# Input rows normalized tile by tile, token halves outermost in the input product, h2 taken ahead of the output sums, and a new list of items for the mixed part

## What is computed

```python
h = rms_norm(x, attn_norm)
proj = h @ w_in                                  # 1024 RWKV columns, then q, k, v of 12 heads, 4 forget logits
y_rwkv = rwkv7_group(proj[..., :1024], ...)      # recurrence over tokens, 4 heads x 64
y_fox  = softmax attention with forget gates     # 4 heads
y_moba = softmax attention on chosen key blocks  # 4 heads
y_sb   = stick-breaking attention                # 4 heads
x = x + concat(y_rwkv, y_fox, y_moba, y_sb) @ w_out
h2 = rms_norm(x, mlp_norm)
x = x + square(relu(h2 @ w_mlp_up)) @ w_mlp_down
```

## Time and profile before

| | us |
|---|---|
| three timed runs, median (lowest to highest) | 1093.09 (1090.01 to 1093.42) |
| the profiled execution | 1084.01 |
| its span, first to last instruction | 1082.4 |
| PE busy in it | 1000.0 (92%) |
| DVE busy | 401.9 (37%) |
| ACT busy | 346.3 (32%) |
| mean granted PE clock | 0.973 |

### The profile page before, as it was taken

The page is one execution under the profiler, slowest core; times in us unless marked ns, Lnnn a source line. Parts: engine busy times, 40 slices in busy tenths (PEclk is TensorE's granted clock), DMA queues, the critical chain, the costliest instruction groups (busy, mean ns, idle before and its releaser), DMA issues.

```text
span 1082.4 us, 20333 instructions
## 1 busy us (share of the span) xinstructions
PE 1000.0 (92%) x8560; PEld 770.7 (71%) x8560; DVE 401.9 (37%) x758; ACT 346.3 (32%) x608; POOL 56.0 (5%) x108
## 2 busy tenths in 40 slices
PE   3999999898997988889969998999999999999998
PEld 3775666556895856566634447999877799997776
DVE  3005142834566565554381125332212142221212
ACT  3001331411333166675460113544211134441110
POOL 0000000112410000002420000000000000000000
PEclk9999999899998899999979998999999999999999
DMA  9011111002000358557988202222122243211222
GB/s 350 23 59 60 59 59 59 33 33 99 7 5 2 92 206 277 161 176 232 348 355 289 91 1 78 79 78 79 39 78 78 78 132 98 84 39 40 81 93 108
DMA packets 57005, 117.46 MB, mean 109 GB/s; under 512 B 4891, under 2 KB 27963, under 8 KB 56787
## 3 DMA queue, kind: packets, MB, share of 16 engines
q1 hardware_dynamic: 50674, 93.05, 25.5%
q0 software_dynamic: 6240, 23.12, 6.2%
HBM read 109.62 MB, written 6.53 MB: 107 GB/s over the span
## 4 chain that ended last, share of the span: by engine, by line
PE 87%; DVE 6%; issue 3%; ACT 2%; DMA 2%; SPq 1%; DVEq 0%; ACTq 0%
PE PS L735 12%; PE PS L1144 11%; PE PS L1145 11%; PE PS L1146 11%; PE PS L817 7%; PE PS L721 6%; PE PS L1114 5%; PE PS L982 3%; PE PS L1217 3%; PE PS L1050 2%; PE PS L1004 2%; PE PS L945 2%; PE PS L739 2%; DMA AR<-in_cache_kv 1%; PE PS L960 1%
## 5 line engine op out<-in xcount | busy, mean ns | idle before, releaser
L2045 DVE TENSOR_TENSOR WL<-Wraw,WH 128x2048 fp32r<-128x2048 f32 x32 | 73.4, 2293 | 164.2 <-ACT WH L1449 164.2
L1144 PE MATMUL PS<-h2H,WH 128*128 128x288 f32 x448 | 132.8, 296 | 0.0
L1145 PE MATMUL PS<-h2L,WH 128*128 128x288 f32 x448 | 132.2, 295 | 0.0
L1146 PE MATMUL PS<-h2H,WL 128*128 128x288 f32 x448 | 131.7, 294 | 0.0
L735 PE MATMUL PS<-W,HM 128*128 128x384 f32 (+1 forms) x384 | 127.2, 493 | 0.0
L1449 ACT ACTIVATE WH<-Wraw 128x2048 fp32r<-128x2048 f32 x32 | 61.0, 1907 | 163.8 <-DMA Wraw<-in_w_mlp_down 140.8
L735 PEld LDWEIGHTS PS<-W,HM 128*128 128x128 f32 x384 | 73.5, 192 | 51.0 <-issue 1.8
L1144 PE MATMUL PS<-WH,uH 128*128 128x512 f32 x256 | 101.4, 396 | 1.8 <-issue 1.8
L1145 PE MATMUL PS<-WL,uH 128*128 128x512 f32 x256 | 99.8, 390 | 0.0
L1146 PE MATMUL PS<-WH,uL 128*128 128x512 f32 x256 | 99.6, 389 | 0.0
L1146 PEld LDWEIGHTS PS<-h2H,WL 128*128 128x128 f32 x448 | 84.4, 188 | 0.0
(11 more groups left out here) (311 smaller groups left out, 1343.4 us busy)
## 6 DMA issues: line engine op xcount, KB each, us to landing
AR<-in_cache_kv SPq DMA_DIRECT2D x76, 384.0 KB, 4.1
AR<-in_cache_kv POOLq DMA_DIRECT2D x44, 384.0 KB, 4.8
Wraw<-in_w_mlp_up SPq DMA_DIRECT2D x16, 1024.0 KB, 5.4
Wraw<-in_w_mlp_down SPq DMA_DIRECT2D x16, 1024.0 KB, 4.9
W<-in_w_in SPq DMA_DIRECT2D x5, 1536.0 KB, 6.5
VQ<-in_x_prompt SPq DMA_DIRECT2D x8, 512.0 KB, 8.0
W<-in_w_in SPq DMA_DIRECT2D x2, 2048.0 KB, 15.7
W<-in_w_out SPq DMA_DIRECT2D x2, 2048.0 KB, 12.7
```

What stands on the lines that cost most here:

```text
L1144: mm(out, lH, rH, start=start, stop=False)
L1145: mm(out, lH, rL, start=False, stop=False)
L1146: return mm(out, lL, rH, start=False, stop=stop)
L2045: tt(WL[:, q % 2, :], Wraw[:, q % 2, :], WH[:, q % 2, :].bitcast(F32), SUB).then_inc(w_lo, 1)
```

## The change

SP's queue: cst and prm, with semaphores of their own (`in_cst`, `in_prm`), go behind the first x tile; W0 comes in two halves of 256 columns (`in_wfirst`, `in_w[0]`) directly behind x, then W1, rc, W2, and last shift0 and the page table, which `in_const` now counts (32 instead of 64, also where POOL waits for it). ACT takes a square root of cleared sums before anything has landed, then squares and root tile by tile. DVE inverts and scales tile i, then evacuates tile i-1. The input product has the token halves outside k; its first block waits for three tiles of hT for half 0 and for five for half 1; its PSUM pairs are turned by two, so that the first block is away from the transposes' banks. DVE takes h2 of tile i-1 ahead of the two output blocks. `PLAN` is another list of the same items.

```diff
--- before.py
+++ after.py
...
@@ -518,15 +521,15 @@
         for n in range(A_FROM):
             ORDER += [("R", n)] + AFTER.get(n, [])
         PLAN = """
-            As0 R23 R24 R25 Ap0 Ay0 R26 R27 As1 R28 R29 Ap1 R30 R31 R32 R33 Ay1 As2 R34 Ap2 R35 R36 Ay2 R37 R38 R39
-            R40 R41 As3 R42 R43 Ap3 R44 R45 Ay3 R46 R47 As4 R48 R49 Ap4 R50 R51 Ay4 R52 R53 As5 R54 R55 Ap5 R56
-            R57 Ay5 R58 R59 R60 R61 B0 As6 R62 Ap6 R63 R64 Ay6 R65 As7 R66 B1 Ap7 R67 R68 Ay7 R69 R70 As8 R71 R72 Ap8
-            R73 R74 Ay8 G0 G1 K0 As9 G2 Ap9 G3 K1 Ay9 G4 As10 K2 K3 Ap10 K4 Ay10 K5 As11 K6 K7 Ap11 K8 Ay11 As12 K9
-            Ap12 K10 K11 Ay12 K12 As13 K13 Ap13 K14 K15 Ay13 K16 As14 K17 K18 Ap14 K19 K20 Ay14 K21 K22 K23 As15 N0
+            As0 R23 R24 R25 Ap0 Ay0 R26 As1 R27 R28 Ap1 R29 Ay1 As2 R30 R31 R32 R33 R34 R35 R36 Ap2 R37 R38 Ay2 R39
+            R40 R41 As3 R42 R43 Ap3 R44 R45 Ay3 R46 R47 As4 R48 R49 Ap4 Ay4 As5 R50 R51 R52 R53 R54 R55 R56 R57 R58
+            Ap5 R59 R60 R61 Ay5 R62 R63 R64 As6 R65 Ap6 Ay6 As7 B0 R66 Ap7 R67 R68 Ay7 B1 R69 R70 As8 R71 R72 Ap8
+            Ay8 R73 R74 As9 G0 G1 Ap9 G2 K0 G3 K1 G4 Ay9 K2 As10 K3 Ap10 Ay10 K4 As11 K5 K6 Ap11 K7 Ay11 K8 As12 K9
+            Ap12 K10 K11 Ay12 K12 K13 As13 K14 Ap13 K15 Ay13 K16 As14 K17 K18 Ap14 K19 Ay14 K20 K21 K22 As15 K23 N0
             S0 Ap15 Ay15 P0 M0 X0 As16 K24 Ap16 K25 K26 Q0 X1 K27 Ay16 K28 K29 As17 K30 Ap17 Ay17 As18 K31 X2 K32
-            Ap18 K33 K34 K35 Ay18 K36 As19 K37 V0 K38 Ap19 V1 K39 Ay19 As20 K40 V2 K41 Ap20 Ay20 As21 V3 K42 Ap21
+            K33 Ap18 K34 K35 Ay18 K36 As19 K37 V0 K38 Ap19 V1 K39 Ay19 As20 K40 K41 Ap20 V2 Ay20 As21 V3 K42 Ap21
             K43 Ay21 K44 V4 V5 K45 K46 As22 V6 K47 Ap22 V7 N1 Ay22 As23 S1 V8 Ap23 Ay23 V9 P1 F0 As24 Ap24 M1 Ay24
-            X3 Q1 As25 X4 Ap25 T0 X5 Ay25 V10 V11 V12 V13 V14 V15 V16 V17 V18 V19 F1 T1
+            X3 Q1 As25 Ap25 X4 X5 Ay25 T0 V10 V11 V12 V13 V14 V15 V16 V17 V18 V19 F1 T1
         """
         KINDS = [t.rstrip("0123456789") for t in PLAN.split()]
         ORDER += [(kind, int(t[len(kind):])) for kind, t in zip(KINDS, PLAN.split())]
@@ -596,15 +599,17 @@
         def _(sp):
             for i, (t0, nr) in enumerate(TILES):
                 sp.dma_start(xin[0:nr, i, :], xrows(i)).then_inc(in_x[i], 16)
-            sp.dma_start(cst[:, :], d["cst"]).then_inc(in_const, 16)
-            sp.dma_start(prm[:, :], d["prm"]).then_inc(in_const, 16)
-            sp.dma_start(small[:, 128:192], d["shift0"]).then_inc(in_const, 16)
-            sp.dma_start(pt_sb[:, :], d["page_table"].rearrange("(o b) n -> o (b n)", o=1)).then_inc(in_const, 16)
-            sp.dma_start(rc[:, :], d["rc"]).then_inc(in_rc, 16)
+                if i == 0:
+                    sp.dma_start(cst[:, :], d["cst"]).then_inc(in_cst, 16)
+                    sp.dma_start(prm[:, :], d["prm"]).then_inc(in_prm, 16)
 
             def load_w(n):
                 if n >= NW:
                     sp.wait_ge(*used(n - NW))
+                if n == 0:
+                    sp.dma_start(wview(0)[:, :, 0:256], pieces[0][:, :, 0:256]).then_inc(in_wfirst, 16)
+                    sp.dma_start(wview(0)[:, :, 256:512], pieces[0][:, :, 256:512]).then_inc(in_w[0], 16)
+                    return
                 sp.dma_start(wview(n), pieces[n]).then_inc(in_w[n % NW], 16)
 
             def load_mlp(q):
@@ -615,9 +620,13 @@
                         sp.wait_ge(*mlp_used(q - 2))
                 sp.dma_start(mlp_view(Wraw, q), mlp[q]).then_inc(in_raw[q % 2], 16)
 
-            for n in range(NW):
+            for n in range(2):
                 load_w(n)
-
+            sp.dma_start(rc[:, :], d["rc"]).then_inc(in_rc, 16)
+            load_w(2)
+
+            sp.dma_start(small[:, 128:192], d["shift0"]).then_inc(in_const, 16)
+            sp.dma_start(pt_sb[:, :], d["page_table"].rearrange("(o b) n -> o (b n)", o=1)).then_inc(in_const, 16)
             sp.wait_ge(xT_ps, 5)
             sp.dma_start(lora[:, 0:256], d["lora_wa"]).then_inc(in_lora, 16)
             sp.dma_start(lora[:, 256:512], d["rwkv_g_up"][0]).then_inc(in_lora, 16)
@@ -630,7 +639,7 @@
             sp.wait_ge(tr_ps, 20)
             sp.wait_ge(k_out, 16 * 10)
             sp.dma_start(X4[:, 0:1024], d["s0"]).then_inc(in_s0, 16)
-            sp.wait_ge(in_const, 16 * 4)
+            sp.wait_ge(in_const, 16 * 2)
             load_forgets(sp, 0, in_lf)
 
             sp.wait_ge(c_ps, AT["U", 1] + 1)
...
@@ -698,7 +707,7 @@
             mm, turn = nc.tensor.matmul, nc.tensor.transpose
 
 
-            pe.wait_ge(in_const, 16 * 4)
+            pe.wait_ge(in_cst, 16)
             for i, (t0, nr) in enumerate(TILES):
                 pe.wait_ge(xs_ready, i + 1)
                 if i >= 2:
@@ -710,14 +719,18 @@
                 last.then_inc(xT_ps, 1)
 
 
-            pe.wait_ge(hT_ready, 5)
             for m in range(8):
-                w_wait(pe, m // 4)
+                if m == 0:
+                    pe.wait_ge(in_wfirst, 16)
+                elif m % 4 == 2 or m == 4:
+                    w_wait(pe, m // 4)
                 if m >= 4:
                     pe.wait_ge(p_ready, m - 3)
-                out = pair(m % 4)
-                for k in range(KT):
-                    for a in range(2):
+                out = pair((m + 2) % 4)
+                for a in range(2):
+                    if m == 0:
+                        pe.wait_ge(hT_ready, (3, 5)[a])
+                    for k in range(KT):
                         last = mm(out[:, a, :], wview(m // 4)[:, k, (m % 4) * 128:(m % 4 + 1) * 128],
                                   hT[:, k, a * 288:(a + 1) * 288], start=(k == 0), stop=(k == KT - 1))
                 last.then_inc(p_ps, 1)
@@ -1237,16 +1250,17 @@
 
 
             act.wait_ge(init, 1)
+            link(f(rstd, ssq, ACT.Sqrt, scale=1.0 / D, bias=eps))
             for i, (t0, nr) in enumerate(TILES):
                 act.wait_ge(in_x[i], 16)
                 f(xs[0:nr, i, :], xin[0:nr, i, :], ACT.Square, accum_out=ssq[0:nr, i:i + 1]).then_inc(squares, 1)
-            act.wait_ge(squares, 5)
-            f(rstd, ssq, ACT.Sqrt, scale=1.0 / D, bias=eps).then_inc(std_ready, 1)
+                act.wait_ge(squares, i + 1)
+                f(rstd[0:nr, i:i + 1], ssq[0:nr, i:i + 1], ACT.Sqrt, scale=1.0 / D, bias=eps[0:nr]).then_inc(std_ready, 1)
 
 
             for m in range(8):
                 act.wait_ge(p_ps, m + 1)
-                f(halves(pT[:, m, :]), pair(m % 4), ACT.Copy).then_inc(p_ready, 1)
+                f(halves(pT[:, m, :]), pair((m + 2) % 4), ACT.Copy).then_inc(p_ready, 1)
 
 
             def take(g):
@@ -1519,12 +1533,6 @@
             link(nc.vector.memset(eps, RMS_EPS))
             link(nc.vector.memset(onec, 1.0))
             nc.vector.memset(gneps, GN_EPS).then_inc(init, 1)
-            dve.wait_ge(in_const, 16 * 4)
-            dve.wait_ge(std_ready, 1)
-            link(recip(rstd, rstd))
-            for i, (t0, nr) in enumerate(TILES):
-                ts(xs[0:nr, i, :], xin[0:nr, i, :], rstd[0:nr, i:i + 1], None, MUL).then_inc(xs_ready, 1)
-
             def take_turned(i, dst, g0, done):
 
                 t0, nr = TILES[i]
@@ -1532,9 +1540,17 @@
                 tt(dst[:, :, t0:t0 + nr], PS[:, base:base + 1024].rearrange("p (k t) -> p k t", k=8)[:, :, 0:nr],
                    prm[:, g0:g0 + 8].unsqueeze(2).to_broadcast([128, 8, nr]), MUL).then_inc(done, 1)
 
-            for i in range(5):
-                dve.wait_ge(xT_ps, i + 1)
-                take_turned(i, hT, C_AN, hT_ready)
+            dve.wait_ge(in_prm, 16)
+            for i, (t0, nr) in enumerate(TILES):
+                dve.wait_ge(std_ready, i + 1)
+                link(recip(rstd[0:nr, i:i + 1], rstd[0:nr, i:i + 1]))
+                ts(xs[0:nr, i, :], xin[0:nr, i, :], rstd[0:nr, i:i + 1], None, MUL).then_inc(xs_ready, 1)
+                if i:
+                    dve.wait_ge(xT_ps, i)
+                    take_turned(i - 1, hT, C_AN, hT_ready)
+            dve.wait_ge(xT_ps, 5)
+            take_turned(4, hT, C_AN, hT_ready)
+            dve.wait_ge(in_const, 16 * 2)
             ts(omka, prm[:, C_KA:C_KA + 2], -1.0, 1.0, MUL, ADD).then_inc(v_step, 1)
             steps[0] += 1
             link(ts(gq, prm[:, C_QN:C_QN + 6], HD ** -0.5, None, MUL))
@@ -2069,10 +2085,10 @@
                 take_output(n)
             for i in range(4):
                 scale_rows(i)
+                if i:
+                    take_h2(i - 1)
                 take_output(2 + 2 * i)
                 take_output(3 + 2 * i)
-                if i:
-                    take_h2(i - 1)
             split_lo(0)
             scale_rows(4)
             split_lo(1)
```

More of the change, by code:

```diff
@@ L273, in build @@
         in_const = sem("in_const")
+        in_cst = sem("in_cst")
+        in_prm = sem("in_prm")
         in_resid = sem("in_resid")
@@ L386, in build @@
         y_ready = sem("y_ready")
+        in_wfirst = sem("in_wfirst")
         in_x = [sem(f"in_x{i}") for i in range(5)]
@@ L682, in _ @@
```

(2 more changed lines are left out.)

## The result

| | us |
|---|---|
| after, median of 4 runs (lowest to highest) | 1073.59 (1071.08 to 1076.10) |
| before in the same comparison, 4 runs | 1091.55 (1089.66 to 1093.42) |
| ratio, with 95% interval | 0.9835 (0.9803 to 0.9868) |
| the profiled execution of after | 1072.73 |
| its span; mean granted clock | 1071.1; 0.970 |

The change takes 18.0 us off. The forecast was 12.8 off, 1080.3, with a range down to 1074.0: the sign and the order of size were right, the time was missed by 6.7 us and the range by 0.4. Of the 6.7, 1.5 is the kernel before itself, whose median is 1091.55 with these runs and not 1093.09; 5.2 is a gain that the sum did not contain.

The account below looks back on a forecast made before the run. PE (TensorE) was taken as busy nearly throughout, so time lay only in its waits or low clock. Terms -6.8 (head), -4.7 (output product to MLP) and -1.3 (middle) summed to -12.8, giving 1080.3 us, range 1074 to 1087.

Parts of the forecast that it names:

- The head: Start of kernel: tile-by-tile roots and table load ahead of x start the input product at 16.75 instead of 23.60, -6.8 us.
- 0.65 later: Head: cst and prm loaded ahead of tiles 1 to 4 delay x by 0.65 us, tile 3 landing at 11.2.
- Rivals 4: Head: the table does not stay, ACT reloads 1.28 us before each Square and Sqrt; +10.1, total 1090.4; chance 0.03.
- 6 (the half piece late): Head: first half piece of weights lands at 19.8 as the whole did; +3.1, total 1083.4; chance 0.03.
- Output product to MLP: Between the products: earlier take_h2 starts PE 3.15 us earlier, plus a kept clock, -4.7; bounds 3.1 to 4.7.
- The middle: Mixed part, 258 to 590 us: the reordered list of items gives -1.3, least certain, from +4 to -5.
- Rival 1: Middle: clock kept in the short steps R58 to R66; middle -4.5, total 1077.1; chance 0.15.
- As15 before K23: Middle: front(15) runs beside K23, so the 1.76 us wait at 445.24 shrinks by about 1.0.
- Rivals 2: Clock low at the starts of both products: +1.7 in head, +1.6 in tail, total 1083.6; chance 0.16.
- Rival 5: Middle: clock stays at 0.50 from R58 until page loads end, about 344 to 400; total 1108; chance 0.04.
- Rival 3: Middle: the list loses, pairs, B1 and late pages at +4 instead of -1.3; total 1085.6; chance 0.11.
- The difference carried over: Whole kernel: timed median 1093.09 lay 9.1 above the profiled 1084.01; added to 1071.2 it gave 1080.3.

Follow-up runs that it names:

- only_head: Kernel before with only the new head and input product (load order, square roots tile by tile, token halves outermost): 1083.32 us, ratio 0.9947.
- after again: The changed kernel, unedited, timed once more beside the kernel before: 1072.06 us, ratio 0.9854.
- before again: The kernel before, unedited, profiled and timed once more: 1089.69 us, ratio 1.0005.
- only_h2: Kernel before with only take_h2 moved ahead of the two output sums: 1085.29 us, ratio 0.9958.
- only_plan: Kernel before with only the whole new list of items (PLAN): 1081.11 us, ratio 0.9932.
- kept_warm: Changed kernel plus two unused 128x512 matmuls filling PE's wait between output product and MLP: 1071.57 us, ratio 0.9837.
- four_moves: Kernel before, old list with K7 behind Ap11, K8 behind Ay11, K23 behind As15, K33 ahead of Ap18: 1083.02 us, ratio 0.9953.
- plan_second: Kernel before with the old list up to Ap8 and the new one behind it: 1084.42 us, ratio 0.9940.
- plan_first: Kernel before with the new list up to Ap8 and the old one behind it: 1088.20 us, ratio 0.9984.
- b1_early: Changed kernel with B1 (DVE's build of queries) back behind R66 instead of behind Ay7: 1070.97 us, ratio 0.9836.

## Why the prediction was wrong by five microseconds

**The head: right, a little too good.** -6.8 forecast, -5.8 timed, and the product starts at 17.1 to 17.8 in five of the six traces with the new head (19.1 in only_head, past the 19 that the forecast named as a sign of being wrong; its slowest x load took 10.8 us), against 23.5 to 25.0 in the seven with the old. The chain was the forecast one: x's last arrivals, root, scaling, one evacuation, eight transposes. The step "0.65 later" for x was too small: the last full tile came at 12.29 and the slowest load took 9.8 us for 8.4, about 1.1 later than my 11.2. Tile 0 also waited for prm until 6.05, but DVE had caught up by 12. The weights were in time, though not by the 2 us that I gave them: the quickest of the four W loads took 11.5 us, and the first half piece was issued at 4.33, so it landed at 15.8 at the earliest, against 14.6; PE never waited. Rivals 4 (a table reload) and 6 (the half piece late) are refuted by the table rows and by PE's product without a wait.

**Output product to MLP: right, 3.2 instead of 4.7 in the trace.** The start is earlier by 3.15, as worked out from the split's end. From there the forecast took the clock as kept; in the trace of after it fell, and 3.1, the bound given with it, is what is left. The 2.35 us forecast from first record to WL with a kept clock is the 2.3 of after again. Timed alone h2 gave -4.6 (-7.1 to -2.2), with an interval too wide to tell 3.1 from 4.7: that it is so near the forecast -4.7 doesn't show the kept clock, and in its own trace the grant fell.

**The middle: the failed step.** Its term was -1.3, and the list gives -7.4 (-10.0 to -4.8) alone, -7.6 as what the other two parts leave of 18.0. By stage, us between first records in PE's timeline (for N1, the last record of its scores), means of four traces with the old list (before, before again, only_head, only_h2) and of four with the new one (only_plan, after, after again, kept_warm):

| stage | old | new | difference | forecast |
|---|---|---|---|---|
| R0 to seq1 | 80.9 | 82.6 | +1.7 | |
| seq1 to U | 14.2 | 9.2 | -5.0 | |
| U to SS | 17.8 | 20.5 | +2.7 | -1.4 for the three |
| SS to the first new keys (N0) | 75.7 | 73.9 | -1.8 | +0.1 |
| N0 to N1 | 93.8 | 92.0 | -1.8 | 0 |
| N1 to output product | 51.5 | 51.5 | 0 | 0 |

Up to SS the bookkeeping was near (-0.6 for -1.4): an Ay straight behind its Ap costs 0.72 and an As straight behind its Ay 0.39 (Ap4 Ay4 As5 in after, for the 0.4 to 0.7 that I took), the 5.51 us went, and the clock fell in the short steps as I had assumed:

```profile
338.00:355.00 17.00, 15.21 (x161) 12.05 (x161) 10.04 (x34) 2.90 (x10) 0.00 (x0) 0.50 0.00 1
```

Rival 1, the clock kept, is refuted by that row; in every other trace with the new first half the grant falls to 0.50 there too, in some with a rise between. What the sum missed stands behind Ap8: -6.5 timed (-9.5 to -3.7) against -1.0. The failed step is the bullet "*As15 before K23*", which counted one displaced K, at the one wait that the earlier trace rows had a row for; K7, K8 and K33 do not occur in the sum at all, so they stood in it at nothing. The rows that I read the earlier trace rows showed 2.8 us of idle in front of 412.0, which I used only as evidence on the clock. Asked of that wait what ends it (DVE's mid and front) and what lies beside it (one K), the new list answers at once: two K's, 1.6 less. A wait of 2.19 us in front of 454.2 (Ap16) shows the limit: in after it is 0.58, at half clock and with the records before it longer, in four_moves it is 2.19 still, and in only_h2, which has the old list and happened to have a low clock there, it is 0.57. A wait that shrinks because PE has become slower is no gain.

The new list also pays for something that neither the sum nor the table shows by itself. From 3 us before N0's scores to 15 us behind, the granted clock is 0.62 to 0.72 in all seven traces with the new second half, 0.81 to 0.85 in five of the six with the old one and 1.00 in four_moves. Why it falls for longer there was not tested.

One thing stays open: how much of the timed gain the traces account for. The stages add up to -4.2, the timed list to -7.4 (-10.0 to -4.8), and the -4.2 leans on one slow trace: SS to N0 is 79.0 in only_h2 and 74.4 to 74.7 in the other three with the old list, and without it the sum is about -3.2. plan_second's trace is 5.5 us below the old mean from R0 to output product for 6.5 timed, but 1.9 of them stand between N1 and the output product, a stretch that takes either 48.8 to 49.9 or 51.6 to 52.3 us, with both lists. The trace of plan_first is 6 us longer than the old mean where twelve runs make it -1.7. Traces with one and the same list differ by up to 6 us in this part (331.5 to 337.2 with the old one), so they place a gain but do not size it: what four_moves shows, 4.2 us of waits gone for 5.1 timed, is the firmest piece, and the rest of the second half's 6.5 is not placed.

**Rivals 2 and 5.** The clock was low over the product's first records in two of six traces with the new head and in two of seven with the old (rows in the last section), so nothing points to an effect of the change; it looks like luck of an execution on either side. Rival 5, 40 us of half clock behind R58, did not come: 17 us. Rival 3 had the wrong sign.

**The difference carried over.** Adding 9.1 us of median over profile to a forecast of 1071.2 was right for before and wrong for after: the profiled execution of after took 1072.73, as nearly forecast, and its median is 0.9 above it. The profile of before was at the short end of runs that spread from 1083 to 1096. The forecast in differences (-12.8) doesn't depend on it, but agreement with the profile of after (1071.2 against 1072.73) would have looked like success while 5 us were missing.

## What to carry to other kernels

In a list that all engines walk, the place of independent PE work counts by itself: put it between the item that gives another engine a long task and the item in which PE needs the result, and look for every wait at such a line, one by one, with the task that ends it and the items beside it. When a change reorders a list, take the largest waits of the old trace in turn and count for each what the new list puts in front of it; "the same items" is no reason for zero. A single profile of a kernel whose executions spread by half a per cent should be set against the median stage by stage before it carries a sum.

## What the hardware showed

**The granted clock ahead of its first change is not to be trusted.** In the trace of b1_early the grant reads 1.00 from the start, but the product's first 8 records take 3.2 us, 0.40 each; in after it is 15 records in the same time and at the same 1.00:

```profile
17.80:21.00 3.20, 3.20 (x8) 2.34 (x8) 0.76 (x2) 0.00 (x0) 0.00 (x0) 1.00 1.05 410
```

```profile
17.40:20.60 3.20, 3.20 (x15) 2.55 (x14) 1.06 (x2) 0.00 (x0) 0.00 (x0) 1.00 1.06 410
```

kept_warm has the same slow start with the fall on record (0.53 from 18.0 to 21.6). The Trainium skill, TensorE: Matmul & The Clock Gate, Part 1, says that throttled is the default and activity releases it, and that the place of the change in a kernel differs from one execution to the next. The slow start of b1_early agrees with both. So a grant of 1.00 ahead of the first change may be no reading of the clock; the durations of the records are. The product takes 1.6 to 2.2 us longer in the four traces that have such a start (b_again, plan_second, b1_early, kept_warm).

**2.10 us of idle go either way.** Behind the same hole of 2.10 us the grant was 0.50 for 3.4 us in after and stayed 1.00 in after again, 1.5 us apart, from the same instructions. A step of a sum that hangs on it is to be given as two values.

**A table load costs its 1.28 us and no more here.** It ran from 0.88 and the dummy root started at 2.17, 1.29 later. The Trainium skill (ScalarE: Activation LUTs, "What ACT_TABLE_LOAD costs") adds a drain of 1.38 us. No such time is seen here, and not for want of work to drain: in the kernel before the load at 12.76 follows right behind five squares, and its square root starts 1.30 later, at 14.06.
